# Two stages of a two-block kernel: the first early expert tiles turned inside the last query step, and the second delta round staged inside the first

## The reference, cut to what matters

```
gc = cumsum(g)                         # gates of the chunk
decay = exp(where(causal, gc_i - gc_j, -inf))
a = where(strict, (k*beta) k^T * decay, 0)
t_inv = inverse(a + I)                 # unit lower triangular
intra = where(causal, q k^T * decay, 0)
k_dec = k * exp(gc_last - gc)
```

```
q = (t @ w_q).reshape(n_tok, 8, 2, 128)
sc = einsum("thpk,hpnk->thpn", q, sub_keys)   # 16 groups of 128 scores
s_top, i_top = top_k(sc, 16); best, pos = top_k(sums of pairs, 16)
idx = chosen experts; g = softmax(best)
act = gelu(einsum("phkd,pd->phk", u_tab[idx], t)); out = einsum(g * act, v_tab[idx])
```

## Time and profile before

| | |
|---|---|
| median of three runs | 2222.3 us (2220.2 to 2222.7) |
| the profiled execution: its time, its span | 2221.12 us, 2219.3 us |
| PE busy | 2104.8 us (95%) |
| DVE, ACT, GpSimd busy | 76%, 37%, 35% |
| mean granted TensorE clock | 0.981 of full speed |

### The profile page before, as it was taken

The page is one execution under the profiler, slowest core; times in us unless marked ns, Lnnn a source line. Parts: engine busy times, 40 slices in busy tenths (PEclk is TensorE's granted clock), DMA queues, the critical chain, the costliest instruction groups (busy, mean ns, idle before and its releaser), DMA issues. The chain is left out here.

```text
span 2219.3 us, 35776 instructions
## 1 busy us (share of the span) xinstructions
PE 2104.8 (95%) x11175; PEld 1854.1 (84%) x11175; DVE 1691.0 (76%) x3372; ACT 831.3 (37%) x1439; POOL 773.3 (35%) x672
## 2 busy tenths in 40 slices
PE   6998978979999998999999999999999999999997
PEld 4886777767888876889899999999998888888886
DVE  3776545677877845899688888888877888888887
ACT  4454422532332324235434444444433333333333
POOL 2000044500000000224388988988853222222221
PEclk9998999999999999999999999999999999999998
DMA  6743100404325215114377988989789999999995
GB/s 135 94 58 39 20 1 0 153 13 121 85 74 131 78 55 183 58 59 135 121 274 248 319 283 298 310 276 314 253 290 346 337 338 336 337 338 338 338 336 200
DMA packets 229811, 428.46 MB, mean 193 GB/s; under 512 B 18500, under 2 KB 155876, under 8 KB 229476
## 3 DMA queue, kind: packets, MB, share of 16 engines
q1 hardware_dynamic: 173108, 255.96, 38.5%
q0 software_dynamic: 41472, 151.01, 19.8%
q10 hardware_dynamic: 15152, 20.51, 2.6%
HBM read 381.28 MB, written 46.14 MB: 193 GB/s over the span
## 5 line engine op out<-in xcount | busy, mean ns | idle before, releaser
L2215 PE MATMUL bank<-u_hi,u_one 128*128 128x512 f32 x768 | 299.1, 389 | 1.6 <-DVE u_two L2335 1.5
L2215 PE MATMUL bank<-u_hi,u_two 128*128 128x512 f32 x768 | 298.8, 389 | 0.0
L2215 PE MATMUL bank<-u_lo,u_one 128*128 128x512 f32 x768 | 298.8, 389 | 0.0
L2198 PE MATMUL bank<-xt_hi,u_hi 128*128 128x384 f32 x832 | 287.1, 345 | 0.0
L2198 PE MATMUL bank<-xt_hi,u_lo 128*128 128x384 f32 x832 | 279.1, 335 | 0.0
L2198 PE MATMUL bank<-xt_lo,u_hi 128*128 128x384 f32 x832 | 278.7, 335 | 0.0
L1950 POOL DMA_INDIRECT row_slot<-in_peer_v_dram,row_index x128 | 141.2, 1103 | 388.0 <-DVE row_x L2343 365.3
L2409 ACT ACTIVATE u_hi<-xh 128x1024 fp32r<-128x1024 f32 x128 | 135.9, 1061 | 330.5 <-PE bank L2215 329.9
L2332 DVE TENSOR_TENSOR u_lo<-xh,u_hi 128x1024 fp32r<-128x1024 f32 x128 | 156.8, 1225 | 80.3 <-ACT u_hi L2409 79.6
L1631 POOL TENSOR_TENSOR k_wlo<-q_raw,k_whi 128x2048 fp32r<-128x2048 f32 x4 | 18.7, 4684 | 469.9 <-ACT k_whi L1761 469.9
L2121 POOL TENSOR_TENSOR u_two<-u_match,u_weight_hi 128x512 fp32r<-128x512 f32 x96 | 164.1, 1709 | 49.7 <-DVE u_match L2261 48.8
(11 more groups left out here) (440 smaller groups left out, 4947.7 us busy)
## 6 DMA issues: line engine op xcount, KB each, us to landing
xh<-in_peer_v_dram SPq DMA_DIRECT2D x128, 512.0 KB, 5.3
xh<-in_peer_u_dram SPq DMA_DIRECT2D x104, 512.0 KB, 4.2
x_raw<-in_w_in_dram SPq DMA_DIRECT2D x56, 512.0 KB, 6.9
v_ga<-acts SPq DMA_DIRECT2D x128, 192.0 KB
acts<-xh ACTq DMA_DIRECT2D x102, 192.0 KB
weights<-u_spread POOLq DMA_DIRECT2D x32, 512.0 KB
v_gg<-weights SPq DMA_DIRECT2D x128, 128.0 KB
p_raw<-in_w_in_dram SPq DMA_DIRECT2D x12, 1024.0 KB, 10.5
```

Of the source, the lines that this page charges most:

```text
L2198: mm = pe.matmul(k.ps[4 + b][:, 0:DENSE], w[b][:, c, :], x[:, c, 0:DENSE], start=(c == 0 and w is uhi and x is hi), stop=(c == DC - 1 and ...
L2215: mm = pe.matmul(k.ps[q][:, :], h[b][:, t * P:(t + 1) * P], w[b][:, f], start=start and h is hhi and w is vhi, stop=stop and h is hlo, ski ...
```

## The change

In `delta_prepare`: DVE's loop is written out. The staging of a round becomes a function `stage`, called for both a ahead of round 0, and for round 1 after level 4 (a = 0) and level 5 (a = 1) of round 0. It spreads the gates first and copies q, k, v after. PE waits for the gates alone ahead of L867, and for the copies ahead of the kk products. v is transposed into b0, not b3, and waits for `diff` instead of `k_kept`. Two waits are added on PE: for `inv_kept` of the round before ahead of the qk products, and for `v_kept` ahead of the transposes of `mt`.

```
+                def stage(i, a):
+                    dve.wait_ge(s["v_turned"][a], after(i))
+                    for h in range(H):
+                        dve.tensor_scalar(gb[a][:, h, :], ...).then_inc(s["staged"][a], 1)
+                    for n, dst in enumerate((qst, kst, vst)):
+                        dve.tensor_copy(dst[a][:, :, :], ...).then_inc(s["staged"][a], 1)
+                for a in range(2):
+                    stage(0, a)
+                for i in range(TT // 2):
...
-                                dve.tensor_tensor(kept["inv"][:, c, :, :], mt[a][:, :, :], b2, ALU.subtract)
+                                dve.tensor_tensor(...).then_inc(s["inv_kept"][a], 1)
+                        if lv in (4, 5) and i + 1 < TT // 2:
+                            stage(i + 1, lv - 4)
...  ACT
-                        act.activation(kept["v"][:, c, :, :], b3, ACT.Copy).then_inc(s["v_kept"][a], 1)
+                        act.activation(kept["v"][:, c, :, :], b0, ACT.Copy).then_inc(s["v_kept"][a], 1)
...  PE
-                            pe.wait_ge(s["staged"][a], after(i * (3 + H) + (3 + H)))
+                            if h == 0:
+                                pe.wait_ge(s["staged"][a], after(i * (3 + H) + H))
                             mm = pe.matmul(b0[:, h, :], gb[a][:, h, :], k.upto[:, :], start=True, stop=True)
...
                         pe.wait_ge(s["m_done"][a], after(i * last))
+                        pe.wait_ge(s["staged"][a], after(i * (3 + H) + (3 + H)))
...  ahead of the qk products
+                        pe.wait_ge(s["inv_kept"][a], after(i))
...  after the transposes of k
-                        pe.wait_ge(s["k_kept"][a], after(i * H + H))
+                        pe.wait_ge(s["diff"][a], after(i * H + H))
                         for h in range(H):
-                            mm = pe.transpose(b3[:, h, :], vst[a][:, h, :], k.ident[:, :])
+                            mm = pe.transpose(b0[:, h, :], vst[a][:, h, :], k.ident[:, :])
...  ahead of the transposes of mt
-                        pe.wait_ge(s["diff"][a], after(i * H + H))
+                        pe.wait_ge(s["v_kept"][a], after(i + 1))
```

```
+        def kept_order(i):
+            return (2, 3, 0, 1) if i == steps - 1 else range(TT)
...  PE
-                turn(0)
-                turn(1)
+                for i in range(steps):
+                    for n in range(per):
+                        if i or n:
+                            pe.wait_ge(q_kept[n], after(i))
+                            queries(i // 2, i % 2, n).then_inc(product[n], 1)
+                        if n == 1:
+                            pe.wait_ge(s["sc_kept"], after(i * 4 + 4))
+                        if n:
+                            scores(i, n - 1)
+                        if i == steps - 1 and n >= 2:
+                            turn(n - 2)
+                    scores(i, per - 1)
                 for e in range(EARLY):
-                    turn(e + 2)
                     pe.wait_ge(u_low, after(e + 1))
...
-                    elif e == 0:
-                        pe.wait_ge(s["sc_kept"], after(4 * (steps + 1)))
+                    else:
+                        pe.wait_ge(s["sc_kept"], after(4 * steps + 1 + e))
...  after the 24 matmuls of M(e)
+                    turn(e + 2)
...  ACT
-                high(2)
-                high(3)
+                highs_at = {(0, 0): 2, (0, 1): 3, (0, 3): 4, (1, 0): 5, (1, 1): 6, (1, 3): 7}
...  after the copy of query product n of step i
-                        if n % 2 and i + 2 < steps:
-                            high(2 * (i + 2) + n // 2)
-                    if i == steps - 1:
-                        copy(0)
+                        if (i, n) in highs_at:
+                            high(highs_at[i, n])
+                        if i == steps - 1 and n == 2:
+                            copy(0)
...
-                    for t in range(TT):
+                    for t in kept_order(i):
```

More of the change, by code:

```diff
@@ L748, in delta_prepare @@
                  "k_turned", "k_kept", "v_turned", "v_kept", "ot_done", "mt_done", "m_turned", "m_done", "x_ready",
-                 "x_kept", "dm_ready", "rate_diff")
+                 "x_kept", "dm_ready", "rate_diff", "inv_kept")
         s = {n: k.sems(f"d_{n}", 2) for n in names}
@@ L755, in _ @@
             def _(dve):
[L756 to L766, removed]
+                def stage(i, a):
+                    dve.wait_ge(s["v_turned"][a], after(i))
+                    for h in range(H):
+                        dve.tensor_scalar(gb[a][:, h, :], k.ones[:, :], g[:, i * 2 + a, h:h + 1], None, ALU.mult
+                                          ).then_inc(s["staged"][a], 1)
+                    for n, dst in enumerate((qst, kst, vst)):
+                        dve.tensor_copy(dst[a][:, :, :], qkv[:, n * H:(n + 1) * H, (i * 2 + a) * P:(i * 2 + a + 1) * P]
+                                        ).then_inc(s["staged"][a], 1)
+                for a in range(2):
+                    stage(0, a)
+                for i in range(TT // 2):
                     for a in range(2):
@@ L807, in _ @@
                             else:
-                                dve.tensor_tensor(kept["inv"][:, c, :, :], mt[a][:, :, :], b2, ALU.subtract)
+                                dve.tensor_tensor(kept["inv"][:, c, :, :], mt[a][:, :, :], b2, ALU.subtract).then_inc(s["inv_kept"][a], 1)
+                        if lv in (4, 5) and i + 1 < TT // 2:
+                            stage(i + 1, lv - 4)
             MT = H + last - 1
@@ L838, in _ @@
                         c = i * 2 + a
-                        b3 = heads(k.ps[4 * a + 3][:, :])
+                        b0, b3 = heads(k.ps[4 * a][:, :]), heads(k.ps[4 * a + 3][:, :])
                         act.wait_ge(s["k_turned"][a], after(i + 1))
@@ L869, in _ @@
                     for a in range(2):
-                        b1, b2, b3 = (heads(k.ps[4 * a + n][:, :]) for n in (1, 2, 3))
+                        b0, b1, b2, b3 = (heads(k.ps[4 * a + n][:, :]) for n in range(4))
                         pe.wait_ge(s["m_done"][a], after(i * last))
+                        pe.wait_ge(s["staged"][a], after(i * (3 + H) + (3 + H)))
                         for h in range(H):
@@ L1703, in _ @@
                         mm.then_inc(s["keys_turned"], 1)
[L1704 to L1713, removed]
                 def turn(e):
@@ L1720, in turn @@
                         pe.wait_ge(u_copied, after(4 * e))
-                    else:
-                        pe.wait_ge(q_kept[0], after(steps))
-                        pe.wait_ge(q_kept[1], after(steps))
                     for c in range(DC):
@@ L1846, in _ @@
                         dve.wait_ge(s["reduced"], after(i - 1))
-                    for t in range(TT):
-                        dve.wait_ge(s["sc_kept"], after(4 * (i + 1) + t + 1))
+                    for n, t in enumerate(kept_order(i)):
+                        dve.wait_ge(s["sc_kept"], after(4 * (i + 1) + n + 1))
                         for g in range(per * t, per * (t + 1)):
```

## The result

The changed kernel takes 2201.3 us (median of four runs, 2199.4 to 2202.5) against 2221.3 of the kernel before (also four; its three shown ahead gave 2222.3): ratio 0.9909, 95% interval 0.9892 to 0.9926. The profiled execution took 2202.5 us, its span is 2200.7 (2219.3 before).

The account below looks back on a forecast made before the run. Barrier-separated stages bind, so savings reach the end; PE bounds the choosing stage but isn't full in delta. Delta 8.6 plus choosing 10.7 gives 19.3 us off 2221.1: 2202 us; likeliest 2198 to 2206, with rivals 1 and 2 2197 to 2210.

Parts of the forecast that it names:

- Turn of the rounds and second round: Delta stage: stagings hidden in DVE's holes, gates first and no pauses for ACT in round 1; gain 6.4 us.
- First round: Delta stage: gates first and no wait of v bring `at` of a = 1 earlier; gain 2.15 us.
- The clock: Delta stage: the granted clock's dip may stay, come twice or go; -1.2, 0 or +1.2 us, taken as 0.
- First scores: Choosing stage, first part: query copy no longer behind the rounding of sections 2 and 3; gain 2.4 us.
- Last step: Choosing stage: turn(0) and turn(1) stand in the step, so M(0) and M(1) start sooner; gain 5.1 us.
- Loop: Choosing stage's early tiles: 4.9 us of waits, mostly for loads, go; two stalls, 1.0 us at M(20) and 0.7 at M(23), come.
- Slack of DVE's choice: Choosing stage: DVE's choice ends 2.6 us before `turn_chosen` wants it.
- the chain of a tile (1): Rival in the early tile loop: each product waits some 0.3 us for the low part; 6.6 us, 2208; chance 0.17.
- The late load or choice and the unhidden staging (2): Rival: load or choice late, or DVE's staging not hidden; 3 to 5 us of gain lost, 2206; chance 0.12.
- 3: Rival: a missed wait keeps the change from working in one stage; half the gain, 2212; chance 0.05.
- 4: Rival, slower: stalls between products drop the granted clock in the early loop; ten products would give 2244; chance 0.03.
- 5: Rival: no change within 0.2%, some later transfer taking the gain all back; chance 0.03.

Follow-up runs that it names:

- Experiment 3: Changed kernel, but round 1 staged after the last inverse of round 0 instead of after levels 4 and 5: 2204.5 us, delta stage 108.0 us.
- experiment 2: Changed kernel, but v transposed into the bank of k again, after ACT has copied k out: 2205.3 us, delta stage 106.4 us.
- Experiment 4: Changed kernel, but round 1 staged after levels 1 and 2 of round 0, beside GpSimd's masks: 2210.5 us, delta stage 112.3 us.
- table in 5: Clock comparison across kernels; its own runs: changed kernel plus 12 filler matmuls on PE per delta round, 2197.5 us, and changed kernel again, 2201.3 us.
- Experiment 7: Changed kernel, but ACT's rounding of the weight sections at its old places: choosing stage 243.5 us, against 240.8 us with the same start.
- Experiment 9: Changed kernel with copy(1) earlier, ACT's exp behind tile 18's gelu, `turn_chosen()` before the `u_low` wait: 2198.9 us; with PE fillers too, 2198.1 us.
- experiment 8: Changed kernel, but GpSimd makes each early tile's low part in four pieces of 256 columns instead of one of 1024: choosing stage 248.9 us.

## Why the prediction was right

2202 was forecast, 2201.3 came. The mechanism was right: both stages ended sooner for the reasons given, and the gains added up. That the total fits within 1 us is partly luck: the steps' sum was 19.3 us, the two stages gave 17.5 in the profiled executions, and 1 us more came from code that wasn't changed. By its steps:

- Turn of the rounds and second round: 6.4 us forecast. From the last `inv` (336.11) to L891 of a = 1 (353.75) it was 17.6 us, now 344.04 - 333.05 = 11.0: 6.6. `at` came at 336.92 and 338.83, which is 340.0 and 341.9 in the old time base, against 340.0 and 342.1 forecast. Experiment 3 gives 2.8 of this to the staging's move and experiment 2 gives 1.8 to v's bank. If these add up, 2.1 us remain that no experiment tells apart: gates ahead of the copies may be one part, and the clock another, which the forecast didn't name. It was 0.86 between the last `inv` and `at` of a = 1 before, and 1.00 after; before, the second gate products and the first kk and qk products took 1.7 us longer than after (a row of this stretch stands in experiment 3). Experiment 4 shows that the staging had to go where GpSimd rests.
- First round: `at` of a = 1 came 12.06 us after the stage's first DVE operation, now 9.91: 2.15, as forecast. The two traces had a like clock there (0.72 and 0.66), so the pair is fair. But this stretch took 8.4 to 10.3 us in the traces of the changed code, by the clock at the stage's start. The forecast had no term for that, and to hit it to the hundredth is luck.
- The clock: 0 was taken between -1.2 and 1.2. In the profiled execution it cost 1.2 us more than before, by a deeper dip in the first round. That is the size which the prediction worked out beside the rule of the Trainium skill ("TensorE: Matmul & The Clock Gate", Part 1: The HAM clock gate), but not its way: the dip that the rule called for in the second round didn't come in this trace. Over executions (table in 5) either kernel meets the dip in either round.
- First scores: 2.4 us forecast; 21.8 us after the first transpose before, 20.0 after: 1.8, as the stretch up to the first product was 0.8 us longer in this execution. Experiment 7 has 2.7.
- Last step: 5.1 forecast, 5.0 measured (from the last scores to M(1), with one turn credited).
- Loop: 4.9 - 1.7 = 3.2 forecast, 2.6 measured. The waits for loads went, as forecast. The two stalls, read as what their periods lost, cost 1.2 us at M(20) (6.20 instead of 5.04) and 0.7 at the list, 1.9 together and not 1.7. Another 0.4 us, taken as 0, was lost over the tiles, 0.2 of it at a GpSimd pass of 2.72 us. (The cover of a tile's chain is 5.83 - 5.65 = 0.18 us by the prediction's own terms, not 0.15.)
- Start of the delta stage and its ends: DVE began 0.4 us sooner after the stage before, and 0.2 us came in small pieces. The forecast had no term for them.
- Slack of DVE's choice: 2.6 forecast, 2.3 measured. Experiment 9 used it up.

The rivals: the chain of a tile (1) was real as a limit (experiment 8) and didn't bind, but for the 0.2 us above. The late load or choice and the unhidden staging (2) didn't come: no wait for a load was left, DVE's choice had 2.3 us of slack, and the holes kept 1.24 and 0.35 us. Nothing spoke for 3, 4 or 5; the granted clock in the loop stayed at 1.00. What 4 feared can happen, though: in experiment 8 a stall of 1.8 us was followed by such a dip, within one product. (M(0) before was 0.8 us longer than 4.25 us, not than twice that, as the prediction's sentence can be read.)

Open: the median fell by 20.0 us, the two stages' rows give 17.5, the means over all traces 18.8 (delta 111.3 and 112.2 against 101.8, choosing 251.1 and 249.5 against 241.4). Stages with the same code vary between executions: the delta stage by 3.4 us, the choosing stage by 1.0, the last from 1111.2 to 1114.3. So the rest isn't told apart.

## What to carry to other kernels

Work moved into an engine's hole needs two checks: that the hole is longer than the work, and that no engine that shares its port is running through there. In this kernel DVE's staging fitted into holes of 3.04 and 2.25 us late in the round, and lost 10 us beside GpSimd's masks (experiment 4). A loop's order is a choice of which chain gets the cover: putting the turn behind the product gave the loads 2 us more and left the tile's own chain 0.2; count both before moving. Where the same code differs by 1.3 or 2.5 us between traces, look at the granted clock first, at the stage's start and behind each pause of PE, and compare stages only between traces with a like clock. Filling a pause can hold the clock; what it is worth in the whole time has to be measured.

## What the runs showed of the hardware

A scaling of 128x128 on DVE (0.28 us alone) waited 10.5 us through a row of back-to-back GpSimd operations of 0.42 us each, to their end (experiment 4). In the same trace DVE's subtractions with both inputs in SBUF got in after each of these operations, at 0.54 us instead of 0.28, and those with one input in PSUM lost nothing (0.69 us). A single GpSimd pass of 2.4 us held DVE's last copies for 2.2 us (experiment 9).

The granted clock fell after stretches in which PE was not idle but sparse, in some executions and not in others: after 2.30 us of work in 4 (changed kernel, 290 to 294 us) it was 0.57 and 0.58 for 8 us, after 1.22 us in 4 (340 to 344 us) it stayed at 1.00. 12 filler calls per round kept it at 1.00 in both traces that had them, four rounds in all. Twelve traces without them had a dip in 16 of 24 rounds. At the start of the delta stage, behind a pause of PE of 3.5 us, the clock was low in every trace, and for a time that differed: 0.80 to 0.83 up to `at` of a = 1 in some, 0.65 to 0.72 in others.
